# Splitting the first conditioning round of a decoder layer into two column halves, with the keys' weights loaded between them

## What is computed

```python
mod = jax.nn.silu(c) @ w_ada + b_ada                 # c: 9 rows (1 prompt, 8 samples); w_ada: 1024 x 6144
sh1, sc1, ga1, sh2, sc2, ga2 = [mm[:, None, :] for mm in jnp.split(mod, 6, axis=-1)]
h = rms_norm(x, g_pre_mix) * (1 + sc1) + sh1
z = h @ w_in                                         # 1024 x 2560: q, k, v, u, s of 512 columns each
zq, zk, zv, zu, zs = jnp.split(z, [ATT_W, 2 * ATT_W, 3 * ATT_W, 3 * ATT_W + SGU_W], axis=-1)
```

## Time and profile before

| | us |
|---|---|
| median of 3 runs | 951.04 |
| lowest, highest | 945.6, 952.12 |
| the profiled execution, whole | 945.78 |
| its span in the trace | 944.1 |
| PE busy | 838.3 |
| DVE busy | 346.7 |
| ACT busy | 209.9 |
| POOL busy | 117.8 |

### The profile page before, as it was taken

One profiled execution on the slowest core, in us unless ns is written; L12 is line 12 of the kernel. 1 busy time (PEld: TensorE's weight loads), 2 busy tenths in 40 slices (PEclk: granted clock), 3 DMA queues, 4 the chain that ended last, 5 costly groups with the idle time before them and its releaser, 6 DMA issues. The chain is left out here.

```text
span 944.1 us, 12190 instructions
## 1 busy us (share of the span) xinstructions
PE 838.3 (89%) x4716; PEld 435.0 (46%) x4716; DVE 346.7 (37%) x842; ACT 209.9 (22%) x437; POOL 117.8 (12%) x190
## 2 busy tenths in 40 slices
PE   4699999997789678999988999479999999999994
PEld 3244444343545455665654555344444444444431
DVE  3203332104778645555451464551003110110137
ACT  4001001102665324333340211011001111111123
POOL 1300000002200112222120010010000000000044
PEclk9799999998789879999998999579999999999997
DMA  8987202644920047999788951419889999999982
GB/s 291 366 280 293 90 17 112 244 163 164 413 60 1 1 152 283 410 420 418 326 352 301 322 215 55 179 47 398 323 301 388 401 418 411 393 411 384 374 278 101
DMA packets 36709, 249.15 MB, mean 264 GB/s; under 512 B 4377, under 2 KB 5785, under 8 KB 23218
## 3 DMA queue, kind: packets, MB, share of 16 engines
q1 hardware_dynamic: 22834, 155.17, 42.2%
q0 software_dynamic: 9376, 81.47, 22.0%
q10 hardware_dynamic: 4448, 11.82, 3.9%
HBM read 231.91 MB, written 16.53 MB: 263 GB/s over the span
## 5 line engine op out<-in xcount | busy, mean ns | idle before, releaser
L769 PE MATMUL ps<-sb 128*128 128x512 f32 x320 | 143.3, 603 | 1.4 <-DVE sb L409 1.4
L2043 PE MATMUL ps<-sb 128*128 128x512 f32 (+1 forms) x256 | 112.9, 594 | 0.0
L769 PEld LDWEIGHTS ps<-sb 128*128 128x128 f32 x320 | 60.3, 193 | 75.7 <-issue 72.6
L1205 PE MATMUL ps<-sb 128*128 128x128 f32 x512 | 66.6, 285 | 19.1 <-ACT sb L1074 9.3
L1205 PEld LDWEIGHTS ps<-sb 128*128 128x128 f32 x512 | 58.1, 146 | 33.5 <-issue 19.2
L1970 DVE TENSOR_TENSOR sb<-sb,ps 128x512 f32<-128x512 f32 (+1 forms) x16 | 10.9, 684 | 161.0 <-PE ps L2043 101.0
L2033 PE MATMUL ps<-sb 128*128 128x512 f32 x144 | 65.7, 610 | 1.0 <-ACT sb L1882 0.9
L2068 PE MATMUL ps<-sb 128*128 128x512 f32 x144 | 63.5, 594 | 0.0
L1725 PE MATMUL ps<-sb 128*128 128x512 f32 x128 | 57.6, 610 | 2.9 <-DVE sb L1484 2.9
L2043 PEld LDWEIGHTS ps<-sb 128*128 128x128 f32 (+1 forms) x256 | 42.0, 167 | 34.0 <-issue 34.0
L957 PE MATMUL ps<-sb 128*128 128x128 f32 (+3 forms) x128 | 49.0, 518 | 3.2 <-ACT sb L870 3.2
(11 more groups left out here) (294 smaller groups left out, 1014.7 us busy)
## 6 DMA issues: line engine op xcount, KB each, us to landing
sb<-in_w_gate SPq DMA_DIRECT2D x16, 2048.0 KB, 19.6
sb<-in_w_up SPq DMA_DIRECT2D x16, 2048.0 KB, 9.4
sb<-in_w_down SPq DMA_DIRECT2D x16, 2048.0 KB, 14.3
sb<-in_w_ada SPq DMA_DIRECT2D x12, 2048.0 KB, 16.8
sb<-in_w_in SPq DMA_DIRECT2D x5, 2048.0 KB, 29.1
y_rows<-sb SPq DMA_DIRECT2D x9, 512.0 KB, 15.6
sb<-in_w_out SPq DMA_DIRECT2D x2, 2048.0 KB, 21.0
sb<-in_x_prompt SPq DMA_DIRECT2D x4, 512.0 KB, 5.4
```

The source lines that it names most:

```text
L769: last = pe.matmul(PS[:, n % 4, :], L.hT[:, k, t * P:t * P + P], w[:, k, :], start=k == 0, stop=k == KC - 1)
L1205: last = pe.transpose(PS[:, h, P * g:P * g + P], kp[:, 4 * (ch % 2) + g, P * h:P * h + P], L.cst("ident"))
L2043: last = pe.matmul(PS[0:n, 1, :], x[:, k, :], w_up[:, k, :], start=k == 0, stop=k == KC - 1)
```

## The change

The first conditioning round's units are cut otherwise: unit j is now one piece of 512 columns of all 1024 rows (eight row blocks of 512 columns, as the `w_in` units are). The pieces are ordered so that units 0 and 1 hold the shift and scale of channels 0 to 511, and units 2 and 3 those of channels 512 to 1023. The load order becomes ada 0, ada 1, keys, ada 2, ada 3, then the rest of `w_in`.

`ada_half` multiplies two units: eight row blocks, two matmuls each, into two of the four 32-row groups of bank 7. `mod_columns` transposes one half of the result after ACT and DVE have each copied 32 rows of it. `modulate` on DVE does for four channel blocks what was done for eight. On PE the order is: half 0 and its columns, then for the keys' tiles 0, 1 and 2 the matmuls of k = 0 to 3, then half 1, then k = 0 to 3 of tile 3, the columns of half 1, and then k = 4 to 7 of all four tiles, with the transposes of finished keys between them as before. `ada_done` is now signalled by half 1. The sum of matmuls of the projection is the same, and rounds 1 and 2 are unchanged.

```diff
--- before.py
+++ after.py
@@ -176,7 +176,9 @@
 LAST_V_SLOT = K_SLOT[0]
 W_OUT = [2, 3]
 EXPERT = [4, 5, 0, 1, 2, 3, 6, 7]
-STATIC = [("ada", 0, j, s) for j, s in enumerate(ADA[0])] + [("win", 0, c, s) for c, s in enumerate(WIN)] + \
+ADA_0 = [("ada", 0, j, s) for j, s in enumerate(ADA[0])]
+WIN_ALL = [("win", 0, c, s) for c, s in enumerate(WIN)]
+STATIC = ADA_0[0:2] + WIN_ALL[0:1] + ADA_0[2:4] + WIN_ALL[1:] + \
          [("ada", r, j, s) for r in (1, 2) for j, s in enumerate(ADA[r])]
 
 
@@ -277,6 +279,7 @@
                                                               "evac_act", "evac_dve"))
         dchain, pchain = self.sem("dve_chain_a"), self.sem("pool_chain_a")
         self.h_ready = self.sem("h_ready")
+        self.half_done, self.half_sb, self.mod_tr = self.sem("half_done"), self.sem("half_sb"), mod_tr
         self.w8_made = self.sem("w8_made")
         self.ws_masked, self.ws_tr, self.wmT_done, self.w8_done = (
             self.sem(n) for n in ("ws_masked", "ws_tr", "wmT_done", "w8_done"))
@@ -358,7 +361,10 @@
                 if t >= 1:
                     evac(t - 1)
             evac(NT - 1)
+            act.wait_ge(self.half_done, 1)
+            act.activation(self.modst[32:64, 0, :], PS[32:64, 7, :], ACT.Copy).then_inc(self.half_sb, 1)
             act.wait_ge(self.ada_done, 1)
+            act.activation(self.modst[96:P, 0, :], PS[96:P, 7, :], ACT.Copy).then_inc(self.half_sb, 1)
             for j in range(4):
                 src = a["b_ada"].rearrange("a (r j n) -> a j r n", r=3, j=4)[:, j]
                 for r in range(1, 3):
@@ -391,26 +397,38 @@
             dve.tensor_copy(self.bsT, PS[:, 5, 3 * KC:4 * KC]).then_inc(self.bs_made, 1)
             link(dve.scalar_tensor_tensor(b_sc, b_sc, 1.0, g_pre, ALU.add, ALU.mult))
 
-            dve.wait_ge(self.ada_done, 1)
-            dve.tensor_copy(self.modst[:, 0, :], PS[:, 7, :]).then_inc(self.mod_sb, 1)
-            dve.wait_ge(mod_tr, 1)
-
             cols = PS[:, 6, :].rearrange("p (k j c) -> p j k c", k=4, j=4)
-            col4 = lambda x: x.rearrange("p (j k) -> p j k", j=2).unsqueeze(3).to_broadcast([P, 2, 4, ADA_SEQS])
-            out4 = lambda x: x.rearrange("p (j k) c -> p j k c", j=2)
-            link(dve.tensor_tensor(out4(scale), cols[:, 2:4, :, 0:ADA_SEQS], col4(g_pre), ALU.mult))
-            dve.tensor_tensor(out4(shift), cols[:, 0:2, :, 0:ADA_SEQS], col4(b_sh), ALU.add).then_inc(cols_ready, 1)
-            link(dve.tensor_tensor(out4(scale), out4(scale), col4(b_sc), ALU.add))
-            dve.wait_ge(cols_ready, 1)
-            dve.wait_ge(ev_a, NT)
-            dve.wait_ge(ev_d, NT)
-            for k in range(KC):
-                h = L.hT[:, k, 0:SEQ]
-                dve.tensor_scalar(h, h, scale[:, k, 0:1], shift[:, k, 0:1], ALU.mult, ALU.add).then_inc(self.h_ready, 1)
+            col = lambda x: x.unsqueeze(2).to_broadcast([P, 4, ADA_SEQS])
             hs = L.hT[:, :, SEQ:TOK].rearrange("p k (b t) -> p k b t", b=SB)
-            by_seq = lambda x: x[:, :, 1:ADA_SEQS].unsqueeze(3).to_broadcast([P, KC, SB, ST])
-            link(dve.tensor_tensor(hs, hs, by_seq(scale), ALU.mult))
-            dve.tensor_tensor(hs, hs, by_seq(shift), ALU.add).then_inc(self.h_ready, 1)
+            by_seq = lambda x: x[:, :, 1:ADA_SEQS].unsqueeze(3).to_broadcast([P, 4, SB, ST])
+
+            def modulate(half):
+
+
+                if half == 0:
+                    dve.wait_ge(self.half_done, 1)
+                    dve.tensor_copy(self.modst[0:32, 0, :], PS[0:32, 7, :]).then_inc(self.half_sb, 1)
+                else:
+                    dve.wait_ge(self.ada_done, 1)
+                    dve.tensor_copy(self.modst[64:96, 0, :], PS[64:96, 7, :]).then_inc(self.mod_sb, 1)
+                dve.wait_ge(mod_tr, half + 1)
+                ks = slice(4 * half, 4 * half + 4)
+                sc, sh = scale[:, ks], shift[:, ks]
+                link(dve.tensor_tensor(sc, cols[:, 2 * half + 1, :, 0:ADA_SEQS], col(g_pre[:, ks]), ALU.mult))
+                dve.tensor_tensor(sh, cols[:, 2 * half, :, 0:ADA_SEQS], col(b_sh[:, ks]), ALU.add).then_inc(cols_ready, 1)
+                link(dve.tensor_tensor(sc, sc, col(b_sc[:, ks]), ALU.add))
+                dve.wait_ge(cols_ready, half + 1)
+                dve.wait_ge(ev_a, NT)
+                dve.wait_ge(ev_d, NT)
+                for k in range(4 * half, 4 * half + 4):
+                    h = L.hT[:, k, 0:SEQ]
+                    dve.tensor_scalar(h, h, scale[:, k, 0:1], shift[:, k, 0:1], ALU.mult, ALU.add
+                                      ).then_inc(self.h_ready, 1)
+                link(dve.tensor_tensor(hs[:, ks], hs[:, ks], by_seq(sc), ALU.mult))
+                dve.tensor_tensor(hs[:, ks], hs[:, ks], by_seq(sh), ALU.add).then_inc(self.h_ready, 1)
+
+            modulate(0)
+            modulate(1)
 
         @block.tensor
         def _(pe):
@@ -433,11 +451,8 @@
                                         xn[t % 2][0:n, P * k:P * k + P], L.cst("ident", n)[:, 0:n])
                 last.then_inc(tr_done, 1)
             pe.wait_ge(silu_c, 1)
-            self.ada_round(pe, 0)
-            pe.wait_ge(self.mod_sb, 1)
-            for k in range(4):
-                last = pe.transpose(PS[:, 6, P * k:P * k + P], self.modst[:, 0, P * k:P * k + P], identity)
-            last.then_inc(mod_tr, 1)
+            self.ada_half(pe, 0)
+            self.mod_columns(pe, 0)
 
     def spatial_mask_dve(self, dve):
 
@@ -485,8 +500,13 @@
     def load_unit(self, sp, unit):
 
 
+
         kind, r, j, slot = unit
-        if kind == "ada":
+        if kind == "ada" and r == 0:
+            c = 1024 * (j % 2) + 512 * (j // 2)
+            src = self.a["w_ada"][0, :, c:c + 512].rearrange("(k p) n -> p k n", p=P)
+            dst = self.L.ring[slot].rearrange("p (k n) -> p k n", k=KC)
+        elif kind == "ada":
             src = self.a["w_ada"][0].rearrange("(k p) n -> p k n", p=P)[:, 2 * j:2 * j + 2, 2048 * r:2048 * (r + 1)]
             dst = self.L.ring[slot].rearrange("p (k n) -> p k n", k=2)
         else:
@@ -495,11 +515,36 @@
             dst = self.L.ring[slot].rearrange("p (k n) -> p k n", k=KC)
         sp.dma_start(dst, src).then_inc(self.ring_full[slot], 16)
 
+    def ada_half(self, pe, half):
+
+
+        slots = ADA[0][2 * half:2 * half + 2]
+        for s in range(2):
+            pe.wait_ge(self.ring_full[slots[s]], 16 * fills("ada", 0, 2 * half + s))
+        w = [self.L.ring[slot].rearrange("p (k n) -> p k n", k=KC) for slot in slots]
+        for k in range(KC):
+            for s in range(2):
+                q = 64 * half + 32 * s
+                ins = pe.matmul(self.PS[q:q + 32, 7, :], self.cS[:, k, 0:32], w[s][:, k, :],
+                                start=k == 0, stop=k == KC - 1)
+        ins.then_inc((self.half_done, self.ada_done)[half], 1)
+
+    def mod_columns(self, pe, half):
+
+
+        pe.wait_ge(self.half_sb, (2, 3)[half])
+        if half:
+            pe.wait_ge(self.mod_sb, 1)
+        q = 64 * half
+        for k in range(4):
+            last = pe.transpose(self.PS[:, 6, P * k + q:P * k + q + 64], self.modst[q:q + 64, 0, P * k:P * k + P],
+                                self.L.at(self.L.CST + q, 64, q, q + 64))
+        last.then_inc(self.mod_tr, 1)
+
     def ada_round(self, pe, r):
 
-        bank, n = 7, ADA_SEQS if r else 32
-        if r:
-            pe.wait_ge(self.mod_sb, 4 * r - 3)
+        bank, n = 7, ADA_SEQS
+        pe.wait_ge(self.mod_sb, 4 * r - 3)
         for u, s in enumerate(ADA[r]):
             pe.wait_ge(self.ring_full[s], 16 * fills("ada", r, u))
             w = self.L.ring[s].rearrange("p (k n) -> p k n", k=2)
@@ -752,22 +797,36 @@
                                             L.cst("ident", r)[:, 0:r])
                 last.then_inc(post_done, 1)
 
+            def product(n, ks):
+
+
+                c, t = groups[n]
+                w = L.ring[WIN[n // NT]].rearrange("p (k n) -> p k n", k=KC)
+                for k in ks:
+                    if n == 0:
+                        pe.wait_ge(self.h_ready, k + 1 + k // 4)
+                    last = pe.matmul(PS[:, n % 4, :], L.hT[:, k, t * P:t * P + P], w[:, k, :],
+                                     start=k == 0, stop=k == KC - 1)
+                return last
+
+            pe.wait_ge(self.ring_full[WIN[0]], 16 * fills("win", 0, 0))
+            for n in range(4):
+                product(n, range(4))
+                if n == 2:
+                    self.ada_half(pe, 1)
+            self.mod_columns(pe, 1)
             for n, (c, t) in enumerate(groups):
                 r = rows(t)
                 slot = WIN[n // NT]
                 if n == 4:
-                    pe.wait_ge(self.h_ready, KC + 1)
-                if t == 0:
+                    pe.wait_ge(self.h_ready, KC + 2)
+                if t == 0 and n:
                     pe.wait_ge(self.ring_full[slot], 16 * fills("win", 0, n // NT))
                 if n >= 4:
                     pe.wait_ge(evac_done, n - 3)
```

(6 more changed lines are left out.)

## The result

Over 22 runs each, the kernel before takes 951.17 us (median; 945.56 to 954.2) and the changed one 955.5 (951.73 to 962.59). The medians are 4.3 us apart; the ratio on record is 1.0051, with a 95% interval of 1.0036 to 1.0066: 4.8 us slower (3.4 to 6.3), where the forecast was 3.2. The profiled execution of after took 956.18 us, its span is 954.2. Beside the trace of before (944.1) that is 10 us more, twice what the medians show. Of these 10, the start accounts for 3.0.

What follows compares the result with a forecast made beforehand. PE, busy 89% of the span, was taken as the bound: tiles start 3.5 us sooner and save 2.4 of low clock, against 6.9 + 0.15 for half 1 and 2.0 for the second chain: +3.2, 954.3 us; range 949 to 965.

Steps and rivals of the forecast that it cites:

- The size and the sign: Whole kernel: +3.2 us, 954.3 against the median; chances faster 0.03, same within about 1% 0.71, slower 0.26.
- Loads: Conditioning loads at the start: 2 KB runs take 5.4 us a unit instead of 4.98, so half 0 starts at 25.3.
- Half 0 and the clock: First conditioning half on PE: 16 steps, starting at half clock, 9.1 us (bounds 6.9 and 13.7), ending at 34.4.
- The rival that two column groups would not bring the clock up: Half 0 stays at 1.2 GHz, 13.7 us instead of 9.1; +10.4 us, 961.5, or 967 for a third; chance 0.27.
- Half 1: Second conditioning half on PE's path behind tiles 0 to 2: 16 steps, 6.9 us, plus 0.15 for mode changes.
- The second chain: Before the tiles' second steps: transposes 0.66 and 1.4 to the first block, a new wait of 2.0 us.
- Cover: Loads of SP, ACT and POOL behind the later ada_done move at no cost; without cover, each late w_in unit up to 5.4 us.
- one to one to the end: PE is full from 72 to 130 us, so the four tiles' later end, +3.2 us, reaches the kernel's end unchanged.

Runs made afterwards that it cites:

- r5: Kernel before with only the first round's conditioning units cut into 2 KB runs, as two 1 MB transfers each; ratio to before 1.0024.
- r3: Kernel after with half 1 moved one tile earlier, behind tile 1, and its columns between tiles 2 and 3; ratio to before 1.0061.
- r7: Kernel after with one unused 512-column matmul behind the x transposes of tile 3 and one behind those of tile 4; ratio to before 1.0036.
- r8: Kernel after with four column groups per half (r2) plus the two extra matmuls of r7; ratio to before 0.9960.
- r2: Kernel after with each half multiplied in four column groups instead of two, even and odd blocks summed when columns are made; ratio to before 0.9963.
- r11: Kernel after, unchanged, profiled a second time; ratio to before 1.0101.
- r10: Kernel after, two column groups, with seven unused matmuls: five before half 0, one behind it, one behind its columns; ratio to before 1.0068.
- r9: The four-group form r2 with seven unused matmuls: five before half 0, one behind it, one behind its columns; ratio to before 0.9999.
- r4_delay4: Kernel before with four unused 512-column matmuls (3.43 us) on PE between the keys' fourth and fifth tile; ratio to before 1.0055.
- r1: Kernel before, unchanged, profiled a second time; ratio 0.9987.
- r6: Kernel before with unused matmuls in PE's first-round waits: three behind units two and three, one behind the last, one behind the column transposes; ratio 0.9967.
- r12: Kernel before with one unused 512-column matmul (0.86 us) on PE between the keys' fourth and fifth tile; ratio to before 1.0027.

## Why the prediction was right

**The size and the sign.** Forecast +3.2 us, most likely within 1%, slower rather than faster. Measured 955.5 against 954.3, in the range, +0.51%, and slower clear of the noise.

**Loads.** 5.4 us a unit was right (r5: 5.38; after: 387 GB/s). The start of half 0 scatters: 23.54 and 24.61 in the two traces of after, 25.02 to 26.04 in r3, r7, r8 and r2. The forecast of 25.3 lies in this spread. The first trace ends the start 0.2 us from the forecast by luck, since two misses cancel: the load came 1.8 us sooner, and the clock fell once more at the first tile, which cost 1.5.

**Half 0 and the clock.** 16 steps, 9.1 us forecast, 9.42, 9.16, 8.38 and 10.00 measured in after, r11, r3, r7. The rival that two column groups would not bring the clock up is refuted: the step went from 0.86 to 0.43 us inside half 0 in after, and r10's half 0 and half 1 (7.06) ran at full clock throughout. What the prediction overlooked is the drop behind the chain; it came in after, r7 and r8 and not in r2, r3 and r11, with the same idle time of PE within 0.03 us, nor in r9 and r10, with matmuls put into it. What decides between the first six is not shown.

**Half 1.** 6.9 + 0.15 forecast, 7.06 measured in every kernel with two groups. It is the largest term on the slower side, and it and half 0 decide: with all four groups in use in both (3.64 and 6.04) r2 is ahead of before.

**The second chain.** 2.0 forecast; 1.66 in after (58.14 to 59.80), with a wait of 1.20 that r3 takes away.

**Cover.** The moved loads of SP, ACT and POOL cost nothing in the stretch that they were argued for: from 75 to 233 us the shift of 3.03 does not change.

**The weak step: one to one to the end.** The prediction called itself wrong if the shift at the fifth tile (its L775) isn't that at the end, and on this point the runs speak against it. At 233 us the shift is still 3.03, so the argument from the earlier trace rows holds as far as it looked, and it looked at 58 us of 900. The measured difference is 4.8 us (3.4 to 6.3), in a second comparison 9.6 (7.8 to 11.4), and the forecast of 3.2 is outside both intervals. This term was sized too small, by 1.6 us and by some 6. The first gap is hardly clear, since the two traces of after and the two of before put the fifth tile 2.4 to 3.6 us apart. The second is clear, and so are those of r3 (fifth tile 0.7 us behind before, 2.9 to 8.6 us slower), r10 (0.7, 4.6 to 8.5) and r9 (4.6 ahead, at most 2.2 faster). r4_delay4, with nothing but 3.4 us of matmuls, gives 5.2 (2.9 to 7.5), which shows neither a surplus nor its absence.

The place where the traces differ is the output projection. In the five traces of before and its near relatives (before, r1, r5, r6, r12) ACT's list of issues lasts 13.5 to 14.6 us and PE's second tile starts 17.5 to 17.6 us behind its first; in the other nine, r4 among them, these are 15.0 to 16.2 and 17.9 to 19.1. From the first tile there to the experts' first gate matmul it is 113.4 to 115.2 us in the five and 115.9 to 120.2 in the nine; from there to the end, 321.6 to 322.4 and 322.0 to 323.9. The stretch from the fifth tile to the output projection scatters too much to tell, 436.5 to 442.7 in the five and 437.9 to 444.9 in the nine. So the long list goes with the halves, whatever the shift of the start, and with r4's plain shift of 3.2 us. Why ACT needs longer is open: no run changed ACT's issues alone. Nor do the ratios follow the single traces well: r2 and r8 have the long list and stand at 0.996, and r7, with the list and the latest start, is only 1.5 to 5.3 us slower than before. So the surplus is shown, its place is likely, and its cause is open.

## What to carry to other kernels

Splitting a small multiplication to start its consumer sooner doubles its price if the split leaves half of TensorE's column groups empty; split it along the contracted rows as well, and let the matmul that moves the result add the parts. Before work is moved, look at the clock in the gaps: a few matmuls of no use in PE's waits (r6) were worth about as much as the best rearrangement (0.9967 beside 0.9960), and in these traces they helped only where they reached close to the next work. A shift of a few us that is exact at the place of the change can still come out as half or as double at the end, so a forecast under 1% should carry that in its range.

## What the runs showed of the hardware

- Extra matmuls that ended early did nothing for half 0: r7's ended 3.3 us before it, and it took 10.0 us (8.4 to 9.4 with none); r10's, up to 24.8, made it 7.06. Each is one trace.
- The clock rose while two of four column groups were at work (4.8 us into half 0 in after) and stayed full through 7.06 us of such work (half 1 in after, both halves in r10).
- The same idle time of PE around the columns (0.84 and 1.29 us) was followed by the low clock in after and r7 and by the full clock in r3 and r11.
- The clock column of the windows reads 1.00 ahead of the first record of the clock, also where steps of 0.85 us show 1.2 GHz (27 to 28 us in after).
- The issue of DMAs is not of fixed length: ACT's eight o_sample loads took 4.21 us in before and 5.21 in after, with the same instructions, and its list of 21 issues there 13.5 to 16.2 us over the 14 traces.
